# Hybrid decoder step on one core: in the sampled attention stage, the exponential, the output copy, its transposes and their reduction change places

## The reference

```
h = rms_norm(x); proj = h @ w_in                 # RG-LRU input, q, k, v, two gates
branch A: causal conv (4) -> RG-LRU scan
branch B: for each of 8 heads two softmax maps (64 dims each), with a relative-position bias:
  p = softmax(q.k/8 + bias, masked);  w = p[0] - lam * p[1];  o = w @ v;  rms_norm(o)
x = x + (sigmoid(gA) * A + sigmoid(gB) * B) @ w_out
up = rms_norm(x) @ w_up; conv (3); gelu(gate) * value; x = x + act @ w_down; final rms_norm
```

## Time and profile before

| what | us |
|---|---|
| median of 3 runs | 2045.7 |
| profiled execution, own time | 2047.13 |
| its span, first to last instruction | 2045.3 |
| PE busy in the span | 1993.9 (97%) |
| DVE busy | 1374.8 (67%) |
| ACT busy | 998.0 (49%) |
| POOL busy | 131.7 (6%) |

### The profile page before, as it was taken

How to read it: one execution, slowest core, us unless ns; L and a number is a source line. 1 busy time by engine, 2 the same in 40 slices (tenths; PEclk the granted TensorE clock), 3 DMA queues, 4 the chain that set the end, 5 groups by cost and what they waited for, 6 DMA issues and landing times. The chain is left out here.

```text
span 2045.3 us, 36009 instructions
## 1 busy us (share of the span) xinstructions
PE 1993.9 (97%) x11888; PEld 1850.7 (90%) x11888; DVE 1374.8 (67%) x2932; ACT 998.0 (49%) x1770; POOL 131.7 (6%) x158
## 2 busy tenths in 40 slices
PE   6999999999999999799999999999999999999998
PEld 6999999999999999688878799999999998989896
DVE  6766676767676767678785476665757474747476
ACT  5756575757565757677874242222313131314133
POOL 0000000000000000145560000000000000000000
PEclk9999999999999999999999999999999999999999
DMA  6411111112121212788873131111112020202012
GB/s 199 144 57 54 57 53 56 53 60 59 50 59 50 59 52 87 262 306 309 310 267 94 37 92 42 53 42 42 52 32 62 22 72 22 72 22 62 14 50 99
DMA packets 167453, 183.26 MB, mean 90 GB/s; under 512 B 11045, under 2 KB 139589, under 8 KB 167349
## 3 DMA queue, kind: packets, MB, share of 16 engines
q1 hardware_dynamic: 166137, 181.24, 27.1%
q10 hardware_dynamic: 1212, 0.81, 0.1%
HBM read 162.82 MB, written 24.46 MB: 92 GB/s over the span
## 5 line engine op out<-in xcount | busy, mean ns | idle before, releaser
L1250 PE MATMUL ps<-h_hi,w_hi 128*128 128x384 f32 (+1 forms) x1152 | 386.9, 336 | 5.0 <-DVEq L967 3.4
L1250 PE MATMUL ps<-h_lo,w_hi 128*128 128x384 f32 (+1 forms) x1152 | 376.7, 327 | 0.0
L1250 PE MATMUL ps<-h_hi,w_lo 128*128 128x384 f32 (+1 forms) x1152 | 376.7, 327 | 0.0
L2456 PE MATMUL ps<-h_hi,f_w_hi 128*128 128x320 f32 (+1 forms) x1136 | 370.7, 326 | 0.8 <-PEq L1579 0.8
L2456 PE MATMUL ps<-h_hi,f_w_lo 128*128 128x320 f32 (+1 forms) x1136 | 370.4, 326 | 0.0
L2456 PE MATMUL ps<-h_lo,f_w_hi 128*128 128x320 f32 (+1 forms) x1136 | 370.2, 326 | 0.0
L2535 ACT ACTIVATE yc<-ps,f_prm 128x384 f32<-128x384 f32 x144 | 93.4, 653 | 555.1 <-PE ps L2456 389.1
L2436 PE MATMUL ps<-d_hi,act 128*128 128x512 f32 x816 | 257.1, 390 | 1.6 <-DVE d_lo L2639 1.6
L1250 PEld LDWEIGHTS ps<-h_hi,w_hi 128*128 128x128 f32 x1152 | 217.2, 189 | 9.1 <-issue 4.0
L1250 PEld LDWEIGHTS ps<-h_lo,w_hi 128*128 128x128 f32 x1152 | 217.2, 189 | 0.6
L1250 PEld LDWEIGHTS ps<-h_hi,w_lo 128*128 128x128 f32 x1152 | 216.9, 188 | 0.0
(11 more groups left out here) (310 smaller groups left out, 3523.7 us busy)
## 6 DMA issues: line engine op xcount, KB each, us to landing
k<-in_cache_k SPq DMA_DIRECT2D x64, 512.0 KB, 5.9
v_raw<-in_cache_v SPq DMA_DIRECT2D x64, 512.0 KB, 4.8
w_raw<-in_w_in SPq DMA_DIRECT2D x48, 512.0 KB, 3.9
f_raw<-in_w_up SPq DMA_DIRECT2D x48, 512.0 KB, 3.9
f_raw<-in_w_down SPq DMA_DIRECT2D x24, 512.0 KB, 3.5
bias<-bias_tiles_dram SPq DMA_DIRECT2D x8, 576.0 KB, 3.8
merged_dram<-mg SPq DMA_DIRECT2D x8, 544.0 KB, 2.7
ow_raw<-in_w_out SPq DMA_DIRECT2D x8, 512.0 KB, 7.6
```

The source lines that it names most:

```text
L1250: last_ = pe.matmul(bank(s)[:, 0:n], w[:, W_SLOT[g], k, :], x[:, k, off:off + n], start=(k == 0 and i == 0), stop=(k == KT - 1 and i == 2))
L2456: l_ = pe.matmul(ps[:, e % 6, 0:n], w[:, p, k, :], x[:, k, off:off + n], start=(k == 0 and i == 0), stop=(k == KT - 1 and i == 2))
```

## The change

Four steps move, and no instruction is added or removed.

- ACT, at h = 1: the exponential comes right behind the keys and queries of that head; the output copy moves from ahead of the exponential (h = 1) to h = 2, behind keys 2 and ahead of the v pages.
- PE: `fold_heads` moves from behind the scores at h = 2 to h = 3, behind K3 and ahead of the `P` by `C` matmuls.
- DVE: `fold_rows` moves from ahead of keys 3 to behind them; in the last body, which has no keys, from h = 2 to h = 3, behind the v page of h = 2.
- DVE: reciprocal, product and `C` move from h = 2 to h = 1, ahead of keys 2; in the last body they were there already.

```diff
 # PE body
+                    if h == 3 and has(b, 2):
+                        fold_heads(b - 1)
                     if h == 3 and has(b, 1):
                         pe.wait_ge(c_done, b)
 ...
                         last.then_inc(qkh_done, 1)
-                    if h == 2 and has(b, 2):
-                        fold_heads(b - 1)
 # ACT body
-                    if h == 1 and has(b, 2):
-                        copy_o2(b - 1)
                     if h == 1 and has(b, 1):
                         act.wait_ge(nmx_done, b)
                         act.activation(P[:, :], P[:, :], ACT.Exp, bias=mx[:, 1:2], accum_out=mx[:, 2:3])\
                             .then_inc(exp_done, 1)
+                    if h == 2 and has(b, 2):
+                        copy_o2(b - 1)
 # DVE body
-                    if h == (2 if isinstance(b, int) and b == DEC_B else 3) and has(b, 2):
-                        fold_rows(b - 2)
                     if has(b, 0) and (h > 0 or at_start(b)):
                         keys(b, h)
+                    if h == 3 and has(b, 2):
+                        fold_rows(b - 2)
 ...
-                    if h == (1 if isinstance(b, int) and b == DEC_B else 2) and has(b, 1):
+                    if h == 1 and has(b, 1):
                         dve.wait_ge(exp_done, b)
```

## The result

The changed kernel takes 2055.11 us in the median (2053.29 to 2055.34, 6 runs), the kernel before 2046.54 (2044.95 to 2048.2, 6 runs): ratio 1.0039, 95% interval 1.0029 to 1.0049, slower by 8.6 us. The forecast was 2054.8, in the range 2050.5 to 2056.6.

The account below looks back on a forecast made before the run. PE was taken to set the 27.50 us pass (26.67 busy). Body 1 0.1, repeated bodies 4.2, last body 3.1 and clock 1.7 sum to 9.1 us, added to the 2045.7 median: 2054.8, range 2050.5 to 2056.6.

Parts of the forecast that it names:

- Repeated bodies: Bodies 2 to 7: K3 earlier, but p_new waits for DVE's reduction behind keys 3; pass 28.2 instead of 27.50, 4.2 us.
- the 0.7 taken: Loss per repeated pass: 0.66 from the late reduction, taken as 0.7 because p_new's weight load is no longer hidden.
- Body 1: No output copy or fold there; only DVE's C block moves ahead of keys 2: between 0 and 0.55, taken as 0.1.
- Last body: Body 8: later copy, and reduction behind DVE's v page 2, which POOL's page 1 holds up; next output tile 3.1 us later.
- The standstill ahead of p_new: Last body: PE finishes the C matmuls and stands still for 2.5 us until the reduction ends.
- The block by POOL: Last body: DVE's two-input page 2 stands fully still during POOL's page 1, taking about 2.8; 3.1 us lost, otherwise 1.5.
- The clock: Behind the last body's PE standstill the granted clock falls to 0.50 for 3.3 to 3.4 us, costing 1.7.
- The rival of 2053.1: The clock does not fall in the last body: 7.4 us in all, 2053.1; chance 0.28.
- its two rows: Clock evidence: a standstill of at least 2.30 us preceded clock 0.50; a stretch with 2.15 of 3.40 busy kept 1.00.
- The case of not slower: Reduction done by 977.8, so each repeated pass gains 0.27, 1.6 in six: 2044.1 to 2045.6; chance 0.05.
- the rival with the 0.7 partly taken back: Later waits absorb part of the repeated bodies' loss: 1.5 to 2.7 instead of 4.2, near 2051.6; chance 0.10.

Follow-up runs that it names:

- e1: The changed kernel with DVE's row reduction put back ahead of keys 3 (last body: ahead of v page 2); 2046.85 us, ratio 0.9999 to the kernel before.
- e4: The kernel before with the changed order in the last body only; 2050.52 us, ratio 1.0019 to the kernel before.
- e7: The kernel before with copy, fold and C moved in the repeated bodies only, reduction left ahead of keys 3; 2044.86 us, ratio 0.9993.
- e3: The changed kernel with the last body's order as in the kernel before; 2050.31 us, ratio 1.0019 to the kernel before.
- e2: The kernel before with only DVE's row reduction moved, behind keys 3 (last body: behind v page 2); 2055.35 us, ratio 1.0038.
- e6: The changed kernel with one added wait: in the last body POOL begins page 1's low part after DVE's page 2; 2051.89 us, ratio 1.0029 to before.
- e5: The kernel before with ACT's exponential moved behind keys 2, output copy left ahead, last body as before; 2042.88 us, ratio 0.9983.

## Why the prediction held, step by step

- **The number: 0.3 from the forecast, closer than its parts.** The forecast was the 2045.7 of three executions and 9.1 for the change. The change measured 8.6 in the medians and 7.9 between the two profiled spans, while the kernel before came out at 2046.54 in six executions, 0.8 higher. The two errors run against each other, which is luck.
- **Repeated bodies: right.** ACT has no idle time from keys 1 on, so its reordering did not make keys 3 late; K3 earlier by 0.98 (1.05 forecast); p_new's wait by DVE's reduction; the pass 28.17 (28.2). The trace prints that wait as 0.71, since it counts from the modelled end of the C matmuls (1.90); counted from where p_new could have started (979.03) it is 0.87, the forecast's "about 0.9". The loss is 0.66 against 0.66 from the replay and the 0.7 taken; over six bodies 3.9 against 4.2. Small differences cancel: the reduction begins 8.86 behind K1 instead of 8.97, since ACT's copy-to-next step took 0.90 instead of 1.05, and from its end to p_new and on to the scores it takes 0.13 and 0.24 instead of 0.06 and 0.20. DVE's C block held keys 2 up by 0.1 and does not enter this.
- **Body 1: 0** against the 0.1 taken. Its K2 has a shift of -0.81, K3 (863.14) one of -0.70, so 0.1 is lost there as replayed; C and p_new behind it are back at -0.76 and -0.85.
- **Last body: right in sum, 3.17 against 3.1, and that in part by luck.** The standstill ahead of p_new was 1.9, not 2.5. Before it PE waited 0.48 for the copy (0.5 forecast), and another 0.5 for `ow_lo` from POOL, 0.9 instead of 0.41, which the prediction did not have. That part comes from the clock in body 7, where it fell in both kernels but at another moment: in the changed kernel it already caught the last transposes of keys, 1.37 to the next matmul instead of 1.00; ACT's next v page came 3.50 later than before and POOL's `ow_lo` 3.51, while PE stood at 3.05. The other traces bear this out. Where those transposes take 1.00 or 1.01 to the next matmul (before, e1, e4 to e7), the matmul that waits for `ow_lo` stands 13.40 to 13.42 behind them, with or without a fall behind; where they take 1.13 (e3), 1.37 (the change) and 1.62 (e2), it stands 13.65, 13.90 and 14.14 behind. No edit isolates it. So of the 3.17 about 0.5 is not the change's, and e4, whose transposes were not caught, shows what is: 2.7 against the 3.1 forecast. The difference is in two terms of the sum: the copy's step took 0.9 instead of 1.05, and POOL's page 1 took 2.35 instead of 2.66. DVE's page 2 ended 1.08 behind POOL's, as before.
- **The block by POOL: right**, and shown by e6. By the Trainium skill's rule (SBUF — State Buffer, "Who interferes with whom") DVE's page 2 had to wait for the whole of POOL's instruction. The trace agrees: 2.53 with it, 1.23 without. The standing still is nearly but not wholly complete, for DVE ends 1.08 behind POOL, 0.15 less than the instruction takes alone.
- **The clock: met in the profiled execution, but not as a fixed price.** It cost 1.65 there (1.7 forecast). Five of six times lie between 2054.54 and 2055.34, with a mean granted clock of 0.995 or 0.996, and one is 2053.29 with 0.997, which would suit an execution without the fall; that one has no profile, and the six times of the kernel before spread 3.3 us, so this is not shown. e4 shows that a wait of the same length can go without the fall. The rival of 2053.1 may therefore be another outcome of the same kernel, and that the forecast took the right one of the two was in part luck: nothing in its two rows, one standstill with a fall and one short wait without, told them apart.
- **The other rivals.** The pass did not take its 0.7 back: the wait ahead of the next pass's first keys is 0.18 as before. The case of not slower gave 0.27 per pass for the reduction done in time; e1 makes that case true and its pass is 27.23, 0.27 shorter. In the rival with the 0.7 partly taken back the prediction has a slip: 6 x 0.25 = 1.5 is what would be taken back, so 2.7 would remain, and the case would run from 2051.6 to 2053.3; the range's lower end of 2050.5 rests on it and stood about 1 us too low. The measured time is far from it.

## What to carry to other kernels

When a step is moved to close a visible wait, look for its last consumer's other inputs. Here the copy, the fold and C were all early enough, and the time was lost at a short reduction that frees a PSUM bank. It had been put behind an instruction of its own engine (DVE) whose input comes from an engine without idle time (ACT), and in the last body behind one that POOL holds up. Replay one pass with each engine's list, starting with the engine that has no idle time; a step behind that engine's tail is late whatever else gets early. Of two steps that stand ahead of the urgent one, the one to move was here the one whose consumer is later: the exponential (e5) gained 3.5 us, where moving the copy (e7) gave 1.5 in the medians, not clear of no change.

## What the runs showed of the hardware

The same PE wait is followed by a fall of the granted clock in one execution and not in another. The wait of 2.40 (2.39 to 2.41) ahead of the last keys of body 7 was followed by 0.50 in the profiled executions of before, of the change, of e2 and of e3, and by 1.00 in those of e1 and e4 to e7; the wait of 1.9 in the last body was followed by a fall in the change and in e2 and not in e4. Where it did not fall in body 7, PE waited 1.0 for DVE's keys a moment later:

```profile
1046.01 1.26 PE L1760 MATMUL ps<-ident,k 128*128 128x128 f32 x8 [2.40 <-DVE kt L2076]
1047.02 1.19 PE L1801 MATMUL ps<-kt,qd 128*128 128x344 f32 x6
...
1050.15 1.22 PE L1801 MATMUL ps<-kt,qd 128*128 128x344 f32 x6 [1.00 <-DVE kt L2076]
```

That is e4. So a fall can be almost free. From those keys to the first output tile it is 8.46 in e4 without the fall (to 1054.47) and 8.73 before with it (1046.07 to 1054.80), 0.3 and not 1.7; and the matmul that waits for `ow_lo` stands 13.42 behind them in both. In the last body, where PE waits for nobody behind p_new, the same fall cost 1.65. What decides between the two outcomes was not settled.

The block of DVE by POOL is not confined to the last body. In the pass of the kernel before, a v page on DVE takes 2.15 beside POOL's and also ends 1.08 behind it:

```profile
988.75 2.15 DVE L2124 TENSOR_TENSOR sv_lo<-v_raw,sv_hi 128x1024 fp32r<-128x1024 f32 x1
```
```profile
987.42 2.40 POOL L1630 TENSOR_TENSOR sv_lo<-v_raw,sv_hi 128x1024 fp32r<-128x1024 f32 x1
```

DVE's keys 3, of which one input lies in PSUM, and the reduction were not held up: in the changed kernel's pass they take their usual 1.29 and 0.28 while POOL's page runs from 977.84 to 980.29.
